# Attention by head pairs in eight slots of the input projection, in a two-layer encoder step on one core

## The chip, the cores and the metric

One Trainium2 chip, one of its cores. The time is the device time of one execution in microseconds (us), the median of several runs. Engines go by the names of the profile: PE (TensorE, its weight loads apart as PEld), DVE (VectorE), ACT (ScalarE), POOL (GpSimd), SP (SyncE, which issues the weight loads).

## What is computed

One step of a hybrid encoder for 256 prompt frames and 64 sample frames, 320 columns together, each of 1,024 numbers. Layer 0 runs two kinds of attention behind one input projection, layer 1 a matrix memory; both have a gated convolutional feed-forward part and an embedding. All is float32. The change lies in layer 0's attention and in the start of the program:

```python
def att_mixer(h, w_in, fox_fb, swa_sink, w_out, fox_cache, swa_cache):
    qa, ka, va, fa, qb, kb, vb = split_cols(h @ w_in, ATT_SIZES)
    logf = jax.nn.log_sigmoid(fa.astype(jnp.float32) + fox_fb.astype(jnp.float32))
    if fox_cache is None:
        oa = fox_prompt(qa, ka, va, logf)
        ob = swa_prompt(qb, kb, vb, sink)
    else:
        oa = fox_sample(qa, ka, va, logf, fox_cache[0], fox_cache[1], fox_cache[2])
        ob, sk, sv = swa_sample(qb, kb, vb, sink, swa_cache[0], swa_cache[1])
    out = jnp.concatenate([oa.reshape(b, S, FOX_HEADS * HEAD_DIM), ob], axis=-1) @ w_out
```

Forgetting attention (fox, 8 heads of 64) is causal softmax attention to whose scores F_q - F_k is added, F being the running sum of logf over cache and frames. Sliding-window attention (swa, 8 query heads on 2 key heads) sees a band of chunks of 64 frames, and its softmax has a sink term in the sum. For the prompt the keys are the prompt's; for the sample a cache of 256 (fox) or 128 (swa) rows comes in front.

## The kernel before, in words

One function, `encoder_step`, holds a block of code for each engine; the engines run through their own lists and wait for each other on counted semaphores. Weights come as units of 128 output columns (512 KB): SP loads unit u into one of four buffers, ACT copies it to a high part (`hi`, L1120), DVE subtracts to get a low part (`lo`, L1399), and PE multiplies in three terms, eight blocks of three matmuls with 320 columns (`block3`, L626 to L628). 270 units make up nearly all of the time.

At the start SP loads the tokens and the first units, ACT and POOL load parameters, caches and embeddings. PE turns the tokens (L690), DVE copies them, ACT and DVE split them (`prenorm`, L1124, and `prenorm_lo`, L1403). `ahead` (L650, L653) runs the first three units block by block behind these, since normalization is applied to the result. `stats` (L668) sums the squares, POOL takes the root (`inverse_rms`, L526), DVE and PE spread it over the columns, and DVE scales the units as it reads them (`in0_read`). The narrow projection (8 columns, weights `wnr`) gives the forget values.

`attention_events` sets the order of the attention on all engines: 48 tasks, one for each kind, head and row tile (two of 128 prompt rows, one of 64 sample rows). A task is `scores` (PE, L854, and L856 for the term of F), the move of the scores with a mask to SBUF and their maximum on DVE (`scores_moved`, L1496 to L1505), the exponential on ACT (`weights`, L1147), the reciprocal sum on DVE and the scaling on POOL or DVE (L552, L1514), transposes on PE three tasks later (`turn`, L880), their copy on ACT (L1157), and `values` (PE, L897) two tasks after that. Projection units 0 to 11 run before the first task; units 12 to 17 are cut in halves and stand between the first 21 tasks; `out_blocks` starts two units of the output projection at the last task. `turn_tok` (L830) turns keys and values for the outputs, `sum_forget` (L809) makes the running sums F on PE. Before unit 4 to 9, `TURNS_AT` places the turns of parameters (`par`), embeddings (`pe`), the narrow projection, and the caches (L768).

The groups that go through PSUM banks 0 to 3 take turns in the order of `group_order`; a group waits until the one four places ahead is read.

## Time and profile before

| | us |
|---|---|
| median of 3 runs | 1197.88 |
| lowest and highest | 1193.0, 1198.23 |
| the profiled execution | 1189.34 |
| span of the profile | 1187.6 |
| PE busy | 1151.6 (97%) |
| PEld busy | 1078.8 (91%) |
| DVE busy | 706.1 (59%) |
| ACT busy | 550.5 (46%) |
| POOL busy | 270.6 (23%) |

The span runs from the first to the last instruction. PE's busy time counts matmuls from start to modelled end, so that they overlap; the distance from one start to the next is the better measure of one. PEclk is the granted clock of TensorE as a share of 2.4 GHz.

### The profile page before, as it was taken

What the parts mean: (1) busy time and instruction counts of PE and PEld (TensorE: products, weight loads), DVE (VectorE), ACT (ScalarE), POOL (GpSimd) and SP (SyncE); (2) the same over time, 40 slices, a digit from 0 to 9 for tenths busy, and PEclk for the clock granted to TensorE, in tenths of its full rate; (3) what the DMA queues carried; (4) which work ended last, traced back from release to release, by engine and by line L of the source; (5) the groups of instructions that cost most, each with busy time, mean ns of one, the idle gap of its engine ahead of it and who ended that gap; (6) DMA issues with size and microseconds to landing.
All of it is one profiled execution on the core that took longest, in us unless ns stands there. A gap on an engine that the chain in (4) does not pass through costs nothing.

```text
span 1187.6 us, 20938 instructions
## 1 busy us (share of the span) xinstructions
PE 1151.6 (97%) x7495; PEld 1078.8 (91%) x7495; DVE 706.1 (59%) x1312; ACT 550.5 (46%) x972; POOL 270.6 (23%) x390
## 2 busy tenths in 40 slices
PE   4999999999999999999999999989999999999998
PEld 3887768899999999999998967789999999999998
DVE  4666653577777775333586546547777777633364
ACT  4244443545555554333462554455555455433343
POOL 5002223422232222000230200234222233200020
PEclk9999967899999999999998999989999999999999
DMA  9431102435555555445355432453555555554541
GB/s 240 127 107 54 54 1 74 120 106 159 169 149 144 156 145 155 146 148 154 107 151 134 108 89 60 80 131 95 166 160 154 147 151 149 149 154 145 157 118 52
DMA packets 283656, 150.41 MB, mean 127 GB/s; under 512 B 7576, under 2 KB 280272, under 8 KB 283600
## 3 DMA queue, kind: packets, MB, share of 16 engines
q1 hardware_dynamic: 278832, 144.20, 42.5%
q0 software_dynamic: 2384, 5.26, 1.9%
q8 instruction: 38, 0.62, 0.2%
q10 hardware_dynamic: 2384, 0.18, 0.2%
q14 instruction: 18, 0.15, 0.0%
HBM read 145.54 MB, written 4.08 MB: 126 GB/s over the span
## 4 chain that ended last, share of the span: by engine, by line
PE 90%; DVE 5%; DMA 2%; ACT 1%; issue 1%; POOL 0%; SPq 0%; ACTq 0%; DVEq 0%
PE bank L626 25%; PE bank L628 24%; PE bank L627 24%; PE bank L854 2%; PE bank L897 2%; PE bank L650 2%; DMA raw<-in_w_att_in 2%; PE bank L653 1%; PE bank L880 1%; PE bank L985 1%; DVE hL L1403 1%; DVE wl L1399 1%; PE bank L668 1%; PE bank L999 1%; ACT wh L1120 1%
## 5 line engine op out<-in xcount | busy, mean ns | idle before, releaser
L1399 DVE TENSOR_TENSOR wl<-raw,wh 128x1024 fp32r<-128x1024 f32 x270 | 333.1, 1234 | 260.5 <-ACT wh L1120 258.3
L626 PE MATMUL bank<-hH,wh 128*128 128x320 f32 x1272 | 399.8, 314 | 0.6 <-ACT Vaug L1271 0.5
L628 PE MATMUL bank<-hH,wl 128*128 128x320 f32 x1272 | 393.9, 310 | 0.0
L627 PE MATMUL bank<-hL,wh 128*128 128x320 f32 x1272 | 393.7, 310 | 0.0
L1120 ACT ACTIVATE wh<-raw 128x1024 fp32r<-128x1024 f32 x270 | 284.3, 1055 | 212.8 <-PE bank L628 186.6
L626 PEld LDWEIGHTS bank<-hH,wh 128*128 128x128 f32 x1272 | 239.5, 188 | 8.0 <-issue 4.5
L627 PEld LDWEIGHTS bank<-hL,wh 128*128 128x128 f32 x1272 | 239.7, 188 | 0.1
L628 PEld LDWEIGHTS bank<-hH,wl 128*128 128x128 f32 x1272 | 239.5, 188 | 0.0
L626 PE MATMUL bank<-hidden_hi,wh 128*128 128x320 f32 x720 | 225.0, 313 | 1.3 <-DVE hidden_lo L1791 1.2
L627 PE MATMUL bank<-hidden_lo,wh 128*128 128x320 f32 x720 | 223.5, 310 | 0.0
L628 PE MATMUL bank<-hidden_hi,wl 128*128 128x320 f32 x720 | 223.4, 310 | 0.0
L626 PEld LDWEIGHTS bank<-hidden_hi,wh 128*128 128x128 f32 x720 | 136.0, 189 | 3.0 <-DVE hidden_lo L1791 1.3
L627 PEld LDWEIGHTS bank<-hidden_lo,wh 128*128 128x128 f32 x720 | 136.2, 189 | 0.0
L628 PEld LDWEIGHTS bank<-hidden_hi,wl 128*128 128x128 f32 x720 | 136.1, 189 | 0.0
L605 POOL TENSOR_TENSOR fb<-cv,us 128x256 f32<-128x256 f32 x64 | 44.3, 691 | 313.8 <-DVE us L1833 198.3
L394 POOL TENSOR_TENSOR sqb<-sqb 128x320 f32<-128x320 f32 x42 | 42.2, 1004 | 207.4 <-ACT sqb L1340 146.0
L1325 ACT ACTIVATE cv<-cv 128x322 f32<-128x322 f32 x64 | 30.4, 474 | 100.8 <-DVE cv L1828 100.8
L1828 DVE SCALAR_TENSOR_TENSOR cv<-gp,PC,cv 128x322 f32<-128x322 f32 x128 | 70.5, 551 | 7.6
L1329 ACT ACTIVATE hidden_hi<-fb 128x320 f32 (+1 forms) x64 | 30.2, 472 | 79.4 <-POOL cs L609 79.4
L609 POOL COPY cs<-gp 128x4 f32 x64 | 63.0, 985 | 0.0
L1837 DVE TENSOR_TENSOR hidden_lo<-fb,hidden_hi 128x320 f32 (+1 forms) x64 | 31.3, 490 | 44.3 <-ACT hidden_hi L1329 44.3
L1322 ACT ACTIVATE cv<-gp,PC 128x322 f32<-128x322 f32 x64 | 42.2, 659 | 22.8 <-DVE gp L1820 20.9
(340 smaller groups left out, 1243.7 us busy)
## 6 DMA issues: line engine op xcount, KB each, us to landing
raw<-in_w_ffn_up SPq DMA_DIRECT2D x128, 512.0 KB, 4.0
raw<-in_w_ffn_down SPq DMA_DIRECT2D x64, 512.0 KB, 4.0
raw<-in_w_rec_in SPq DMA_DIRECT2D x24, 512.0 KB, 3.9
raw<-in_w_att_in SPq DMA_DIRECT2D x18, 512.0 KB, 4.1
raw<-in_w_ple_gate SPq DMA_DIRECT2D x16, 512.0 KB, 4.1
raw<-in_w_att_out SPq DMA_DIRECT2D x8, 512.0 KB, 3.8
raw<-in_w_rec_out SPq DMA_DIRECT2D x8, 512.0 KB, 3.9
raw<-in_w_ple SPq DMA_DIRECT2D x4, 512.0 KB, 3.5
```

The costliest lines, as they stand in the source:

```text
L394: ops.tensor_tensor(sqb[:, 0, :], sqb[:, 0, :], sqb[:, j, :], ALU.add).then_inc(sem("sq_added"), 1)
L605: g.tensor_tensor(fb[:, s, 0:TP], cv[:, s, 0:TP], us[:, s, 0:TP], ALU.mult)
L609: g.tensor_copy(dst, tail).then_inc(sem(f"f{l}"), 1)
L626: mmul(out, a, rh[:, k, :], start=first and k == 0, stop=False)
L627: mmul(out, a, rl[:, k, :], start=False, stop=False)
L628: m = mmul(out, b, rh[:, k, :], start=False, stop=last and k == 7)
L1120: A(wh[:, u % R, :], raw[:, u % R, :], ACT.Copy).then_inc(hi_ready, 1)
L1322: A(cv[:, s, :], gp[:, s, 2:T + 4], ACT.Identity, scale=PC[:, l, bass.ds(j + 64, 1)], bias=PC[:, l, bass.ds(j + 96, 1)]).then_inc(sem(f"cv ...
L1325: A(cv[:, s, :], cv[:, s, :], ACT.Gelu_apprx_tanh).then_inc(sem(f"gelu{l}"), 1)
L1399: V.tensor_tensor(wl[:, u % R, :], raw[:, u % R, :], wh[:, u % R, :].bitcast(F32), ALU.subtract).then_inc(lo_ready, 1)
L1828: V.scalar_tensor_tensor(out=cv[:, s, :], in0=gp[:, s, tap:tap + T + 2], scalar=PC[:, l, bass.ds(j + 32 * tap, 1)], in1=cv[:, s, :], op0=A ...
L1837: V.tensor_tensor(FL[:, bass.ds(j, 1), :].rearrange("p a t -> p (a t)"), fb[:, s, :], FH[:, bass.ds(j, 1), :].rearrange("p a t -> p (a t)" ...
```

## The change

Units are put in another order: keys and values of the swa heads, then their queries, then query, key and value of each fox pair (`ATT_COLS`). The attention has eight slots, one for a pair of heads, swa first (s = 0 to 3), and in each both heads, the two prompt tiles and the sample rows are done at once. The events are `u` (a whole projection unit), `S` (scores), `norm` (scaling), `PT` (turned weights), `PV` (values), `o` (the output split), `vt` and `kt` (values and keys turned), `lf` (forget values). Score banks are 4, 5 (prompt rows of the two heads) and 6 (sample rows of both, with the queries in a block-diagonal tile `QB`, which POOL writes); values use bank 7. DVE moves a slot's scores in five pieces with one operation each, which adds the mask, turns the sign and keeps the minimum. The swa sink is no extra column any more, but a term of the sum. F comes from scans on DVE, and F_q is left out, since softmax does not change by it; the term of F_k is put into the banks ahead of the scores.

At the start, `ahead` takes two units; ACT does all its splits before the squares; POOL makes its constants first and begins its loads when weight unit 2 has landed, the two narrow weights and layer 0's convolution parameters among them, which ACT loaded before. The root of the first normalization stands on POOL in the middle of the loads. PE runs 16 matmuls on constants before the tokens land, and three behind each token tile from the fourth on. Three output units instead of two are started in the last slots, block by block in the order of `K_ORDER`.

```diff
-ATT_COLS = [P * j for j in range(12)] + [1544 + P * j for j in range(6)]
+ATT_COLS = [2056, 2184] + [1544 + P * p for p in range(4)] + [512 * j + P * p for p in range(4) for j in range(3)]
...
-SKEW_T, SKEW_V = 3, 5
...
-HALF_AT = [0, 2, 4, 6, 8, 10, 12, 14, 16, 18, 19, 20]
-TOK_AT = [1, 2, 3, 21, 24, 25]
...
-OUT_FROM = len(TASKS) - 1
+FIRST = 2
+WARM = 16
+
+
+K_ORDER = [4, 5, 6, 7, 0, 1, 2, 3]
...
+    e = [("par", 0), ("par", 2), ("par", 3), ("cache", 4), ("u", 4), ("pe", 0), ("pe", 1), ("u", 5),
+         ("S", 0), ("pe", 2), ("pe", 3), ("vt", 0), ("u", 6), ("norm", 0), ("narrow", 0), ("cache", 0), ("cache", 1),
+         ("PT", 0), ("S", 1), ("u", 7), ("norm", 1), ("PV", 0), ("cache", 2), ("cache", 3), ("o", 0), ("u", 8),
+         ("PT", 1), ("S", 2), ("lf", 0), ("u", 9), ("norm", 2), ("PV", 1), ("vt", 1), ("o", 1), ("u", 10)]
+    for s in range(2, 6):
+        e += [("PT", s), ("S", s + 1), ("u", 2 * s + 7), ("norm", s + 1), ("PV", s)]
+        e += [("vt", (0, 0, 0, 2, 3, 4)[s])] if s > 2 else []
+        e += [("o", s)] + ([("u", 2 * s + 8)] if s < 5 else [])
+    e += [("kt", 0), ("kt", 1), ("PT", 6), ("S", 7), ("kt", 2), ("kt", 3), ("kt", 4)]
+    e += [("out", k) for k in range(4)] + [("norm", 7), ("PV", 6), ("o", 6), ("out", 4), ("out", 5), ("PT", 7), ("out", 6), ("PV", 7), ("o", 7)]
+    return e
...
+def group_banks():
+
+    fixed = {("pt_e", 7): 4, ("pt_o", 7): 5, ("pt_s", 7): 6}
+    fixed.update({("o", s): 7 for s in range(8)})
+    banks, turn, last, previous = [], 0, {}, []
+    for n, key in enumerate(group_order()):
+        b = fixed.get(key)
+        if b is None:
+            b, turn = turn % 4, turn + 1
+        banks.append(b)
+        previous.append(last.get(b))
+        last[b] = n
+    return banks, previous
...
+            link(g.memset(MS[:], 0.0))
+            link(g.tensor_copy(MS[0:64, TP:T], MFox[0:64, 256:320]))
+            link(g.tensor_copy(MS[64:128, TP:T], MFox[64:128, 320:384]))
+            g.memset(QB[:], 0.0)
...
+            g.memset(gp[:], 0.0).then_inc(sem("const2"), 1)
+
+            def inverse_rms(stage):
+                pool.wait_ge(sem("ms"), NORMS[stage] + 1)
+                g.tensor_tensor(rcol[:], ms[:], cst[:, 2:5], ALU.pow).then_inc(sem("rcol"), 1)
+
+            par0, par, ld_pe, ld_cache = sem("ld_par0"), sem("ld_par1"), sem("ld_pe"), sem("ld_cache")
+            pool.wait_ge(raw_landed[2], 16)
+            for i, nm in enumerate(("w_att_in", "w_rec_in")):
+                c = (1536, 2048)[i]
+                pool.dma_start(wnr[:, i], I[nm][0][:, c:c + 8].rearrange("(k p) c -> p k c", p=P)).then_inc(sem("ld_narrow"), 16)
+            pool.dma_start(prow[0:96, 0, :], I["ffn_conv_w"][0].rearrange("t (j c) -> (t j) c", c=P)).then_inc(par0, 16)
...
+            inverse_rms("mixpre0")
...
+            for i in range(WARM):
+                mmul(bank[7][:, 0:P], ones[:], ident[:], start=True, stop=True)
...
+                if j >= 3:
+                    for i in range(3):
+                        mmul(bank[7][:, 0:P], ones[:], ident[:], start=True, stop=True)
...
+                ahead([UNITS["in0"] + i for i in range(FIRST)], [gid("in0", i) for i in range(FIRST)], hH, hL,
+                      *prenorm_waits("mixpre0"))
+                in_unit(0, 2, lambda k: stats("mixpre0") if k == 5 else None)
+                in_unit(0, 3, rms_at("mixpre0", 6))
...
+                    elif name in ("vt", "kt"):
+                        turn_tok(name, i)
+                    elif name == "S":
+                        scores(i)
+                    elif name == "PT":
+                        turn_weights(i)
+                    elif name == "PV":
+                        values(i)
+                    elif name == "out":
+                        out_blocks(0, i)
+                for at in range(7):
+                    out_block(0, 2, at)
+                out_blocks(0, 7)
+                out_block(0, 2, 7)
+
+            def turn_cache(j):
+
+                gi = gid("cache", j)
+                bank_free(pe, gi)
+                pe.wait_ge(sem("ld_cache"), 16 * 6)
+                for t in range(2 if j < 4 else 1):
+                    m = trans(gbank(gi)[:, t * P:(t + 1) * P], kcache[:, t, j * P:(j + 1) * P] if j < 4 else kcs[:], ident[:])
+                m.then_inc(done(gi), 1)
...
+                    trans(gbank(gi)[0:n, t * 8:t * 8 + 8], lfz[0][:, t0:t0 + n], ident[0:8, 0:8])
+                for t in range(2):
+                    m = trans(gbank(gi)[0:8, 64 + t * P:64 + (t + 1) * P], clf[:, t, :], ident[:])
+                m.then_inc(done(gi), 1)
...
+            def scores(s):
+
+                fox, p = s > 3, s % 4
+                if s:
+                    pe.wait_ge(sem("s_moved"), 5 * s)
...
+                    for t in range(2):
+                        for half in range(2):
+                            hf, h = 64 * half, 2 * p + half
+                            mmul(bank[4 + half][:, t * P:t * P + (t + 1) * P], selR[hf:hf + 40, h:h + 1].to_broadcast([40, P]),
+                                 FrowR[hf:hf + 40, 0:(t + 1) * P], start=t == 0, stop=False, skip_group_check=True)
+                    mmul(bank[6][:, 0:T], selS[:, 2 * p:2 * p + 2, :].rearrange("p a b -> p (a b)"), FrowR[0:40, TP:TP + T],
+                         start=True, stop=False, skip_group_check=True)
+                for t in range(2):
+                    for half in range(2):
+                        hf = 64 * half
+                        m = mmul(bank[4 + half][:, t * P:t * P + (t + 1) * P], q[hf:hf + 64, t * P:(t + 1) * P], k[hf:hf + 64, 0:(t + 1) * P],
+                                 start=not fox and t == 0, stop=True, skip_group_check=True)
+                        if t:
+                            m.then_inc(sem("s_done"), 1)
+                pe.wait_ge(sem("queries"), 2 * s + 2)
+                mmul(bank[6][:, 0:w], QB[:, s, :], kc, start=not fox, stop=True, skip_group_check=True)
+                mmul(bank[6][:, w:w + TS], QB[:, s, :], k[:, TP:T], start=False, stop=True, skip_group_check=True).then_inc(sem("s_done"), 1)
...
+            def turn_weights(s):
+
+                b = s % 2
+                for half in range(2):
+                    gi = gid(("pt_e", "pt_o")[half], s)
...
+                    pe.wait_ge(sem("p_ready"), 5 * s + 2 * half + 2)
+                    for i, c in enumerate((0, P, 2 * P)):
+                        m = trans(gbank(gi)[:, i * P:(i + 1) * P], S_sb[:, b, 384 * half + c:384 * half + c + P], ident[:])
+                    m.then_inc(done(gi), 1)
...
+            def values(s):
+
...
+                for t in range(2):
+                    for half in range(2):
+                        hf, W = 64 * half, (PTe, PTo)[half]
+                        mmul(gbank(gi)[hf:hf + 64, t * P:TP], V[:, t, c[half]:c[half] + 64], W[:, 2 * t * P:2 * t * P + (2 - t) * P],
+                             start=t == 0, stop=t == 1)
...
+            def weights(s):
+
+                b = s % 2
+                for i, (_, _, c, w) in enumerate(pieces(s)):
+                    act.wait_ge(sem("s_moved"), 5 * s + i + 1)
+                    A(S_sb[:, b, c:c + w], S_sb[:, b, c:c + w], ACT.Exp, scale=-1.0, bias=nmax[:, b, i:i + 1],
+                      accum_out=aden[:, b, i:i + 1]).then_inc(sem("s_exp"), 1)
...
+                    A(hH[:, j, :], xT[:, j, :], ACT.Copy, scale=NC[:, 0, 64 + j:65 + j]).then_inc(sem("h_hi"), 1)
+                    if j == 3:
+                        hi(1)
...
+                for j in range(KT):
+                    A(sqb[:, j, :], xT[:, j, :], ACT.Square).then_inc(sem("sq"), 1)
+                    if j == 3:
+                        hi(3)
...
+            def scores_moved(s):
+
+                fox, b = s > 3, s % 2
...
+                masks = [MFox[:, 2 * P:], MFox[:, P:]] * 2 + [MS[:]] if fox else [MSwa[:, P:], MSwa[:]] * 2 + [MFox[:, 0:P + TS]]
+                for i, (bk, c0, c, w) in enumerate(pieces(s)):
+                    if i % 2 == 0:
+                        dve.wait_ge(sem("s_done"), 3 * s + i // 2 + 1)
+                    V.tensor_tensor_reduce(out=S_sb[:, b, c:c + w], in0=bank[bk][:, c0:c0 + w], in1=masks[i], scale=-1.0,
+                                           scalar=3e38 if fox else nsink5[:, s, i:i + 1], op0=ALU.add, op1=ALU.min,
+                                           accum_out=nmax[:, b, i:i + 1]).then_inc(sem("s_moved"), 1)
...
+            def normalise(s):
+
+                b = s % 2
+                dve.wait_ge(sem("s_exp"), 5 * s + 5)
...
+                V.reciprocal(ainv[:, b, :], aden[:, b, :]).then_inc(sem("a_inv"), 1)
+                dve.wait_ge(sem("a_inv"), 2 * s + 2 if s < 4 else s + 5)
+                for i, (_, _, c, w) in enumerate(pieces(s)):
+                    V.tensor_scalar(S_sb[:, b, c:c + w], S_sb[:, b, c:c + w], ainv[:, b, i:i + 1], None, ALU.mult).then_inc(sem("p_ready"), 1)
```

The first place is POOL's list at the start (`DMA` is the issue of a transfer; `clf` and `sinkb` are the last of six cache loads, `gp` the last constant, `rcol` the root). Before:

```order
L498 DMA clf<-in_cache_fox_logf 128x2x8
L499 DMA sinkb<-in_swa_sink 128x8
L501 MEMSET Ut 128x128
L502 AFFINE_SELECT Ut<-Ut 128x128 [waits const_step]
...
L515 MEMSET gp 128x648 [waits const_step]
L526 TENSOR_TENSOR rcol<-ms,cst 128x3 [waits ms]
L521 DMA out_s_swa_k<-kcs 64x128 [waits ld_cache]
```

Now:

```order
L508 MEMSET gp 128x648 [waits const_step]
L518 DMA wnr<-in_w_att_in 128x8x8 [waits raw_landed2]
L518 DMA wnr<-in_w_rec_in 128x8x8
L519 DMA prow<-in_ffn_conv_w 96x128
...
L526 DMA nrow<-in_rec_norm 8x128
L512 TENSOR_TENSOR rcol<-ms,cst 128x3 [waits ms]
L529 DMA petok<-in_p_prompt 128x2x256
...
L538 DMA clf<-in_cache_fox_logf 128x2x8
L539 DMA sinkb<-in_swa_sink 128x8
L545 DMA out_s_swa_k<-kcs 64x128 [waits ld_cache]
```

The constants stand ahead of the loads, the loads begin behind a wait for weight unit 2, and the root has moved from behind all of them to a place ahead of 13: four of embeddings (`petok`), three of biases and six of caches, in their old order.

The second place is PE's list where projection unit 3 ends and unit 4 begins (`prow`, `nrow` are parameter rows, `kcs` the swa key cache). Before:

```order
L702 MATMUL bank<-ident,prow 128x128 [waits in_read0,ld_par1]
L702 MATMUL bank<-ident,nrow 128x104 [waits in_read0]
L626 MATMUL bank<-hH,wh 128x320 [waits lo_ready,in_read0]
L627 MATMUL bank<-hL,wh 128x320
L628 MATMUL bank<-hH,wl 128x320
```

Now:

```order
L732 MATMUL bank<-ident,prow 128x128 [waits in_read0,ld_par0]
L732 MATMUL bank<-ident,prow 128x128 [waits in_read0,ld_par1]
L732 MATMUL bank<-ident,nrow 128x104 [waits in_read0]
L826 MATMUL bank<-ident,kcs 128x128 [waits ld_cache,in_read0]
L656 MATMUL bank<-hH,wh 128x320 [waits lo_ready,par_in]
L657 MATMUL bank<-hL,wh 128x320
L658 MATMUL bank<-hH,wl 128x320
```

The turn of the key cache, with its wait for the cache loads, has moved ahead of unit 4; it stood ahead of unit 9, with the same wait ahead of unit 8.

The third place is PE's list amid the fox heads (`S_sb` are weights to be turned, `FrowR` and `selR` or `selS` give the term of F, `hH` and `wh` belong to a projection unit). Before, the small matmuls of several tasks stood between two halves of a unit:

```order
L830 MATMUL bank<-ident,kT 128x128 [waits in_read0,tok_read]
L830 MATMUL bank<-ident,kT 128x128 x3
L854 MATMUL bank<-kT,mix 128x128 [waits s_moved]
L856 MATMUL bank<-FrowR,selR 128x128
L880 MATMUL bank<-ident,S_sb 128x128 [waits p_ready]
L830 MATMUL bank<-ident,kT 64x128 [waits in_read0,tok_read]
L830 MATMUL bank<-ident,kT 64x128 x3
L854 MATMUL bank<-kT,mix 128x256 [waits s_moved]
L856 MATMUL bank<-FrowR,selR 128x256
L626 MATMUL bank<-hH,wh 128x320 [waits lo_ready,in_read0]
L627 MATMUL bank<-hL,wh 128x320
L628 MATMUL bank<-hH,wl 128x320
```

Now the last turns of slot 4 and all scores of slot 5, with a whole unit behind them:

```order
L904 MATMUL bank<-ident,S_sb 128x128 [waits p_ready,vt_read]
L904 MATMUL bank<-ident,S_sb 128x128
L905 MATMUL bank<-ident,S_sb 64x128
L874 MATMUL bank<-FrowR,selR 128x128 [waits in_read0,s_moved]
L874 MATMUL bank<-FrowR,selR 128x128
L874 MATMUL bank<-FrowR,selR 128x256 x2
L876 MATMUL bank<-FrowR,selS 128x320
L881 MATMUL bank<-kT,mix 128x128 x2
L881 MATMUL bank<-kT,mix 128x256 x2
L886 MATMUL bank<-kcT,QB 128x256 [waits queries]
L887 MATMUL bank<-kT,QB 128x64
L656 MATMUL bank<-hH,wh 128x320 [waits lo_ready,in_read0]
```

The matmuls of one slot now stand together, with a wait at their head and one ahead of `QB`.

## Rows read from the trace of the kernel before

**Rows 1.** Busy by stage: stretch, its length, then each engine's busy us, PEclk, DMA share.

```profile
42.80:82.00 39.20, 39.13 (x270) 35.56 (x270) 23.56 (x43) 12.04 (x13) 1.29 (x2) 1.00 0.45 120
82.00:143.00 61.00, 60.32 (x384) 45.73 (x384) 39.35 (x98) 30.57 (x89) 11.35 (x15) 1.00 0.24 70
143.00:157.00 14.00, 12.70 (x81) 8.10 (x81) 9.98 (x46) 8.53 (x36) 4.89 (x7) 1.00 0.01 3
157.00:190.00 33.00, 33.00 (x123) 20.53 (x122) 15.54 (x68) 12.96 (x58) 10.03 (x14) 0.50 0.01 5
...
221.50:238.40 16.90, 13.90 (x76) 12.65 (x74) 13.56 (x22) 9.29 (x21) 11.11 (x11) 0.80 0.21 62
```

**Rows 2.** The chain that ended last, its beginning: start us, us, what.

```profile
3.84 17.98 DMA raw<-in_w_att_in
...
24.30 0.87 PE bank L650 x2
...
37.41 1.81 POOL rcol L526
...
42.84 0.42 PE bank L626
...
221.61 1.37 PE bank L668 x12
```

**Rows 3.** Timeline of PE, one weight block of an output unit: start us, us.

```profile
198.13 0.31 PE L626 MATMUL bank<-hidden_hi,wh 128*128 128x320 f32 x1
...
198.57 0.31 PE L626 MATMUL bank<-hidden_hi,wh 128*128 128x320 f32 x1
```

**Rows 4.** Timeline of PE, attention matmuls among projection blocks.

```profile
84.14 0.48 PE L854 MATMUL bank<-kT,mix 64*128 64x128 f32 x2
84.38 0.30 PE L856 MATMUL bank<-FrowR,selR 40*128 40x128 f32 x1
...
86.57 0.70 PE L854 MATMUL bank<-kT,mix 64*128 64x256 f32 x2
86.92 0.47 PE L856 MATMUL bank<-FrowR,selR 40*128 40x256 f32 x1
87.32 0.66 PE L830 MATMUL bank<-ident,kT 128*128 128x128 f32 x4
87.91 0.64 PE L854 MATMUL bank<-kcT,mix 64*64 64x256 f32 x2
...
110.66 0.27 PE L897 MATMUL bank<-PT,Vtok 64*64 64x64 f32 x1
110.67 0.43 PE L854 MATMUL bank<-kcT,mix 64*64 64x256 f32 x1
```

**Rows 5.** Groups of DVE by shape, 41 to 222 us (busy us, mean ns | idle before).

```profile
L1399 DVE TENSOR_TENSOR wl<-raw,wh 128x1024 fp32r<-128x1024 f32 x24 | 29.5, 1228 | 21.4 <-ACT wh L1120 21.4
...
L1505 DVE TENSOR_REDUCE amax<-S_sb 128x1 f32<-128x256 f32 x8 | 3.4, 420 | 0.3
...
L1501 DVE TENSOR_TENSOR S_sb<-bank,MSwa 128x256 f32<-128x256 f32 x8 | 3.3, 413 | 0.0
...
L1590 DVE TENSOR_TENSOR peL<-pef,peH 128x1280 fp32r<-128x1280 f32 x1 | 1.5, 1492 | 0.0
```

**Rows 6.** Timeline of POOL, the first and last of 13 load issues.

```profile
6.23 0.77 POOL L489 DMA_DIRECT2D petok<-in_p_prompt  x1
...
13.58 0.56 POOL L499 DMA_DIRECT2D sinkb<-in_swa_sink  x1
```

**Rows 7.** DMA issues of 0 to 60 us: KB each, us to landing.

```profile
wnr<-in_w_rec_in ACTq DMA_DIRECT2D x1, 32.0 KB, 15.3
...
out_s_swa_v<-vcs POOLq DMA_DIRECT2D x1, 32.0 KB, 2.8
...
sinkb<-in_swa_sink POOLq DMA_DIRECT2D x1, 4.0 KB, 7.0
```

More of the change, by code:

```diff
@@ L638, in unit @@
                         hook(k)
-                    block3(u, k, out, rh, rl, first, last)
+                    block3(u, k, out, rh, rl, first and k == 0, last and k == 7, k == 7)
             def ahead(us, gs, rh, rl, hi_wait, lo_wait):
@@ L1455, in narrow @@
                 s = sem(f"narrow_step{l}")
-                scaled(l, 0, z[:, 0, :], rows=slice(0, 8), last=False, name=f"narrow{l}").then_inc(s, 1)
+                scaled(l, 0, z[0], rows=slice(0, 8), last=False, name=f"narrow{l}").then_inc(s, 1)
                 dve.wait_ge(s, 1)
@@ L1727, in input_recurrent @@
                     elif name == "narrow":
-                        narrow(1, mz)
+                        narrow(1, [mz[:, i, :] for i in range(3)])
                     elif name == "half":
```

819 lines of the change are left out of this document (368 added, 451 removed).

## The prediction

> **What bounds the kernel now.** The profiled execution took 1189.34 us by its own clock, 1187.6 us of it span; the three timed runs have a median of 1197.88 us, 8.5 us more. I sum against the profile and put the difference on the median. A change of 0.5% (6 us) is about the least that a measurement of this kernel can tell from none.
>
> I read the busy times by stage first, because the change lies wholly between the start and the sum of squares behind the first output projection. From 42.80 to 190 us TensorE is called busy almost throughout [rows 1], but two things are to be seen. In the stretch from 82 to 143 us its weight loads fall far behind its matmuls, since the small attention matmuls come between the projection's. And once projection blocks have run out, TensorE has gaps (12.70 of 14 us busy), and in the next 33 us the granted clock is 0.50, the lower level of 1.2 GHz [rows 1]. So the attention stage is bound by TensorE's own instruction list, half of the time at half speed; VectorE is busy 39.35 of 61 us there, and is not the bound.
>
> Then the chain that ended last, at its beginning [rows 2]: it hangs on a weight transfer that lands at 21.84 us, passes to TensorE at 24.30, to the root on GpSimd at 37.41, to the fifth projection unit at 42.84, and reaches the sum of squares of the output projection at 221.61. The stretch that the change rewrites is therefore 221.61 - 42.84 = 178.8 us, with the start ahead of it.
>
> **Part 1: the start.** The loads of GpSimd's queue, some 2 MB, now wait until weight unit 2 has landed. Before, the tokens, three units and these loads, 4.8 MB, took the 17.98 us of the chain's transfer [rows 2], 0.27 MB per us. The tokens and two units are 2.25 MB: 8.4 us by that rate, so both are there at some 12 us. FIRST = 2 needs no third unit. Behind ScalarE's copy and the split of 1.23 us [rows 5] on VectorE, I put the first projection matmul at 14.5 us instead of 24.30. Before, from there to the start of the root was 13.1 us, with three units in front of it. The changed order has two units, five blocks of the third, then the sum of squares, which waits a little for its additions; I take 12.2 us, and with the root's 1.81 us [rows 2] it ends at 28.5 us, 10.7 us sooner.
>
> But this gain is not kept. GpSimd now issues the last 13 loads behind the root, and TensorE wants the turned sliding-window cache, which waits for all six cache loads, ahead of unit 4 (before, this wait stood ahead of unit 8). The same 13 issues took from 6.23 to 14.14 us [rows 6], 7.9 us, so the last goes out at 36.4. It needs 2.8 us at least (a small store in a quiet stretch) and 7.0 at most (the same load when the queues were full) [rows 7]; the queues then carry four weight units beside it, so I take 4.2. Unit 4 starts at 40.8 us, 2.0 us sooner; bounds 39 and 44. TensorE stands idle from about 33 to there. In the stretch from 221.5 us, which also holds an idle engine, the mean clock was 0.80 of 16.9 us [rows 1], 3.4 us lost, so between 0 and 3.4 us is lost behind this wait; I take 2. **The start comes to nothing: -2.0 + 2 = 0**, with ends -4 and +5. The warming matmuls on TensorE cost nothing: nothing can run there before the tokens land. The two narrow weight loads move from ScalarE's queue to GpSimd's, behind unit 2, and VectorE waits for them ahead of the mean square; before they needed up to 15.3 us [rows 7], with full queues. Issued at 13 to 16 us they land between 17 and 30; only past 24 do they delay the root. That makes the upper end +5 rather than +1. The constants, now ahead of the loads on GpSimd, are done before unit 2 lands.
>
> **Part 2: the work from unit 4 on.** All of it is TensorE's list, at full clock. A block of three is 0.44 us [rows 3], so a unit of 24 is 3.53; 14 input and 8 output units are 77.6 us, unchanged. 50 transposes (embeddings, caches, keys and values) at 0.59/4 = 0.15 [rows 4] are 7.5, the narrow projection 24 x 0.147 = 3.5, the turned forget values 0.8: 11.8 together. The 15 forget sums on TensorE go; the three scans that replace them run on VectorE, where a whole slot covers them.
>
> A slot: scores of 128 columns cost 0.24, of 256 columns 0.35, a row-sum matmul of 256 columns 0.40 [rows 4]; 64 columns have no row and lie between 0 and 0.24, I take 0.20; values go by the same widths. A banded slot: scores 2 x 0.24 + 2 x 0.35 + 0.24 + 0.20 = 1.62, eight transposes 1.20, values 2 x 0.35 + 2 x 0.24 + 4 x 0.20 = 1.98; 4.8 us. A forget slot: row sums 2 x 0.24 + 2 x 0.40 + 0.45 = 1.73, scores 1.73, nine transposes 1.35, values 1.18 + 6 x 0.20 = 2.38; 7.2 us. Four of each: **48.0 us**.
>
> The two heads of a pair use different halves of the array's rows. Twice at full clock a matmul on 64 rows begins with its neighbour: 110.66 and 110.67 us [rows 4]. So part of each pair overlaps; I take off 4 us, between 0 and 10. TensorE: Matmul & The Clock Gate in the Trainium skill, section "Why this matters for your kernels", says that small matmuls in distinct row groups, or in distinct column groups, run at the same time; by it the values would overlap as well, and this is the second rival.
>
> Hand-overs between units and attention I put at 3 us, from none to 6.
>
> Stalls: a slot's scores are moved by five fused operations on VectorE. The row does not exist before; for 256 columns it costs at least the plain move, 0.41, and at most move and reduction, 0.83 [rows 5]. Taking 0.5 on average, 2.5 us, the exponentials follow behind, the unit's read and split take 2.9 us after the unit, the scaling 2.0: weights are ready some 7.5 us after the scores. TensorE has 3.53 + about 2 + 0.45 + 3.53 = 9.5 us of other work there, so nothing is lost; at 0.83 per piece, 9.1, still covered. GpSimd's copies of queries and doubled keys are needed 10 us after the cache wait and take 4. One place is not covered: slot 0's weights. Behind its scaling VectorE still has the split of the embeddings, 1.49 us [rows 5], the four narrow steps and two cache copies, and the banks of the second and third turn are freed by these: 8.5 us of VectorE after unit 6, against 4.1 + 0.4 on TensorE. 4 us stall, between 1 and 8; 1 us more for the rest. The tail is covered too: slots 6 and 7 have key turns and output blocks between them.
>
> Sum: 77.6 + 11.8 + 48.0 - 4 + 3 + 5 = 141.4 us in place of 178.8: **-37.4 us**. With the start at 0 the profile would be 1152 us, the median 1160.5. The ends are from -47 (start -4, overlap 10) to -19 (start +5, no overlap, 4 us more of stalls, hand-overs +3, and 2 us of VectorE in the slots).
>
> Where it comes from: half clock in 33 us [rows 1] lost 16.5; the 48 attention tasks, at full clock, took the rest of the stretch, 178.8 - 16.5 - 77.6 - 14 = 70.7 us (14 for the turns, the narrow projection and some 2 us of forget sums), against 48.0 - 4 + 5 + 3 = 52.
>
> **Rivals.** *The caches come later.* If the narrow weights land past 24 us, or the last load needs 7 us, unit 4 starts at 47, the clock loss is 3.4, and the first slot waits 8. For it: every load is issued behind one on the same queue, and the root stands between. Against it: far less traffic at that time. 6.2 + 1.4 + 4 = 12 us more than forecast: 1172. Chance 0.17.
>
> *Pairs run wholly together.* Scores and values of two heads at once: per banded slot 0.59 + 1.0 less, per forget slot 0.59 + 0.64 + 1.2; 16 us in all, where I took 4. Time 1148.5. For it: the shared starts [rows 4]; against it: consecutive value matmuls in the rows of before never show it. Chance 0.17. By the rule of that page the row and the column halves would overlap, and this is what it would give.
>
> *The clock falls and stays, slower than before.* Place: the idle before unit 4, then the many waits in slots. Price: work at 1.2 GHz takes twice its time, so each us spent at half speed costs half of it. It decides from 2 x 37 = 74 us spent at the lower level between 41 and 185 us; 100 us of it gives 1211. For it: it fell after 14 us with 1.3 us of gaps [rows 1]. Against it: there were no projection blocks then, while from 82 to 143, where they are interleaved as now, it stayed at 1.00. Chance 0.05.
>
> *The slots do not shorten anything*, because stalls fill what TensorE saves: within 6 us of before. Chance 0.03; nothing in VectorE's load speaks for it.
>
> **How the numbers follow.** My forecast (1151 to 1169, chance 0.58) gives 1160.5. To hold the time 8 times in 10 the range goes from 1145, which takes in the overlapping pairs, to 1179, past the late caches. Faster by over 0.5%: 0.58 + 0.17 + 0.17 = 0.92; same 0.03; slower 0.05.
>
> **What would show it.** In the changed profile: the first projection matmul near 14.5 us; the root near 28; a gap on TensorE from 33 to 41 put down to the cache load, with a fall of the clock behind it; a stall of some 4 us at slot 0's turned weights; clock at 1.00 from 50 us to the sum of squares; that sum near 185 instead of 221.61. Wrong would be: a gap elsewhere of over 3 us, half clock inside the slots, a fused move over 1 us, or unit 4 before 36 us.

## The result, and the profile after

The changed kernel takes 1137.65 us (median of 4 runs, 1137.24 to 1139.77); the kernel before, beside it, 1197.86 (1193.0 to 1198.23). The ratio on record is 0.9534, 95% interval 0.9479 to 0.9588; the kernel before spreads by several us (see the last experiment), and the quotient of these two medians alone is 0.9497. The forecast was 1160.5, its range 1145 to 1179: the direction was right, and the time lies 7 us below the range. The profiled execution took 1137.24 us, 52.1 less than the one before; the forecast for it was 37.4 less.

The busy times by stage of the changed kernel, to be held against [rows 1] (stretch, its length, then each engine's busy us, the granted clock, DMA share, GB/s):

```profile
33.50:42.20 8.70, 0.52 (x3) 0.50 (x3) 2.92 (x6) 0.00 (x0) 3.52 (x7) 0.70 1.11 305
42.20:50.00 7.80, 7.80 (x37) 7.33 (x37) 3.62 (x13) 1.06 (x1) 4.05 (x12) 0.67 0.07 19
...
58.00:66.70 8.70, 6.03 (x43) 4.17 (x41) 6.47 (x16) 3.04 (x5) 0.47 (x2) 1.00 0.27 72
66.70:80.00 13.30, 13.28 (x92) 11.97 (x94) 7.87 (x27) 8.72 (x20) 0.00 (x0) 0.87 0.15 41
80.00:95.00 15.00, 15.00 (x120) 13.55 (x119) 12.54 (x40) 9.44 (x31) 1.74 (x4) 1.00 0.32 84
95.00:110.00 15.00, 14.98 (x123) 13.42 (x123) 10.45 (x30) 8.32 (x27) 1.40 (x2) 1.00 0.32 94
110.00:127.00 17.00, 17.00 (x140) 15.45 (x138) 10.71 (x32) 8.46 (x24) 0.46 (x2) 1.00 0.32 93
127.00:150.00 23.00, 21.00 (x180) 18.40 (x179) 10.53 (x40) 11.28 (x41) 4.68 (x8) 1.00 0.37 113
```

The 33 us at 0.50 are gone: from 80 us to the sum of squares the clock is 1.00. What is left is a hole ahead of 42 us, a mean clock of 0.67 behind it, a smaller hole at 58 to 66.7 us with a clock of 0.87 behind it, and 2 us without work between 127 and 150 us. The chain that ended last shows the first two holes, and answers to [rows 2] (start us, us, what):

```profile
26.94 1.80 POOL rcol L512
...
36.14 5.45 DMA sinkb<-in_swa_sink
...
41.73 0.45 PE bank L826
42.18 0.29 PE bank L656
...
63.38 1.40 DVE peL L1617
...
66.33 0.34 DVE kcT L1645
...
66.72 0.33 PE bank L904
```

The root ends at 28.74, the last load goes out at 36.14, lands 5.45 later, and unit 4 begins at 42.18. In slot 0 the embeddings' split and a cache copy stand ahead of the third turn. The sum of squares of the output projection, at 221.61 in [rows 2], begins at 172.57.

| | forecast | measured |
|---|---|---|
| first projection matmul | 14.5 | 15.95 |
| root ends | 28.5 | 28.74 |
| unit 4 begins | 40.8 | 42.18 |
| from there to the sum of squares | 141.4 + 2 | 130.4 |
| from there to the end of the span | 966.0, as before | 962.8 |

One fox slot of the changed kernel on TensorE's timeline (start us, us; each score or value matmul of the program shows up as two passes, and a row is one pass or several that follow each other):

```profile
112.87 0.82 PE L897 MATMUL bank<-ident,S_sb 128*128 128x128 f32 x6
...
113.95 0.50 PE L874 MATMUL bank<-FrowR,selR 40*128 40x128 f32 x4
...
114.29 0.95 PE L881 MATMUL bank<-kT,mix 64*128 64x128 f32 x8
115.17 0.70 PE L886 MATMUL bank<-kcT,QB 128*128 128x256 f32 x2
...
115.84 0.40 PE L656 MATMUL bank<-hH,wh 128*128 128x320 f32 x1
...
119.54 0.43 PE L920 MATMUL bank<-PTe,Vtok 128*64 128x256 f32 x1
119.55 0.43 PE L920 MATMUL bank<-PTo,Vtok 128*64 128x256 f32 x1
...
120.24 0.40 PE L932 MATMUL bank<-PTs,vcache 128*64 128x64 f32 x8
...
120.83 0.44 PE L847 MATMUL bank<-ident,sqb 128*128 128x128 f32 x2
```

The first passes of the two heads' values begin 0.01 us apart, as the two matmuls at 110.66 and 110.67 us do in [rows 4]. The slot takes 115.84 - 112.87 = 2.97 and 120.83 - 119.54 = 1.29, together 4.26 us; the forecast had 7.2 before its deduction for overlap. A banded slot, measured in the same way, takes 2.28 + 1.18 = 3.46, against 4.8.

### The profile page after: what moved, and what is told of

The parts are those of the page before. It is cut to its first block, busy times and chain, and to the rows that moved or that the text cites. A ratio compares the mean times of both kernels' runs of the same rounds, so it can differ in the third digit from the quotient of the medians.

```text
span 1135.4 us, 20638 instructions
## 1 busy us (share of the span) xinstructions
PE 1101.6 (97%) x7433; PEld 1056.6 (93%) x7433; DVE 689.1 (61%) x1274; ACT 540.8 (48%) x932; POOL 258.1 (23%) x386
## 4 chain that ended last, share of the span: by engine, by line
PE 90%; DVE 5%; ACT 2%; POOL 1%; issue 1%; DMA 0%; ACTq 0%; DVEq 0%; POOLq 0%
PE bank L656 26%; PE bank L658 25%; PE bank L657 25%; PE bank L680 2%; PE bank L683 1%; PE bank L1020 1%; DVE hL L1437 1%; ACT wh L1151 1%; DVE wl L1433 1%; PE bank L698 1%; PE bank L1034 1%; PE bank L720 1%; DVE xT L1467 1%; DVE hidden_lo L1910 1%; PE bank L706 1%
```

## Experiments

Two lengths are compared throughout: the moment at which VectorE takes the mean square of the output projection (223.0 us in the kernel before, 174.0 in the changed one), which closes the rewritten stretch, and the length of layer 1's mixer from its first mean square to the one behind its output projection (171.6 and 168.5 us), whose instructions no version touches.

| kernel | median us (lowest to highest) | mean square at | layer 1's mixer |
|---|---|---|---|
| changed | 1137.65 (1137.24 to 1139.77) | 174.0 | 168.5 |
| heads apart | 1143.82 (1141.91 to 1146.37) | 177.5 | 170.0 |
| same half | 1153.34 (1152.27 to 1154.34) | 187.9 | 171.6 |
| units ahead | 1153.19 (1152.51 to 1153.88) | 190.6 | 168.5 |
| moved twice | 1146.6 (1146.5 to 1147.25) | 182.7 | 168.5 |
| no warming | 1137.65 (1137.08 to 1141.21) | 174.9 | 171.6 |
| caches first | 1131.27 (1130.03 to 1134.31) | 168.6 | 168.5 |
| slot 0 freed | 1142.13 (1141.62 to 1144.12) | 175.6 | 173.1 |
| slot 0 freed, caches in twos | 1136.25 (1136.24 to 1138.32) | 169.9 | 171.6 |
| caches first, unit 4 first, slot 0 freed | 1123.05 (1122.01 to 1128.62) | 159.1 | 168.5 |

### Do the two heads of a pair run at the same time?

First the heads one behind the other, in row sums, scores and values alike:

```diff
-                for t in range(2):
-                    for half in range(2):
+                for half in range(2):
+                    for t in range(2):
```

> Same instructions as the changed kernel, but in scores, row sums and values of a slot all matmuls of the first head stand ahead of those of the second, so that neighbours use the same half of the array. Theory A (the neighbours of a pair run at the same time, and that is what the forecast priced too low): the prompt's values cost 0.71 us more per slot, the sample's about 0.4, the scores about 0.3 (2 x 0.24 + 2 x 0.35 = 1.18 one after the other, against 0.86 in the changed kernel's trace); 1.2 to 1.6 us in each of eight slots, 10 to 13 us in all: 1147 to 1151 us, and no two value matmuls begin within 0.02 us of each other. Theory B (the small matmuls are cheap in any order, and the rows of before were too dear because TensorE waited there for its weight loads): 1137 to 1140 us.

Measured: 1143.82 us, and the mean square 3.5 us later. Both theories missed, and the timeline says why (a banded slot's values):

```profile
96.85 0.43 PE L920 MATMUL bank<-PTe,Stok 128*64 128x256 f32 x1
96.86 0.43 PE L920 MATMUL bank<-PTo,Stok 128*64 128x256 f32 x1
97.12 0.38 PE L920 MATMUL bank<-PTe,Stok 128*64 128x256 f32 x1
97.13 0.38 PE L920 MATMUL bank<-PTo,Stok 128*64 128x256 f32 x1
97.33 0.27 PE L920 MATMUL bank<-PTe,Stok 128*64 128x128 f32 x1
...
97.55 0.28 PE L932 MATMUL bank<-PTs,vcs 128*64 128x64 f32 x2
98.01 0.33 PE L932 MATMUL bank<-PTs,vcs 128*64 128x64 f32 x2
```

Here the program has PTe 256, PTe 128, PTo 256, PTo 128, and still PTo's first matmul begins with PTe's first, ahead of PTe 128 at 97.33 us. So the engine starts a matmul for the other column half although one for the first half is still waiting ahead of it. The prompt's values take 0.70 us in either order, the scores some 0.86; overlap was lost by the sample's values, 0.5 us in a banded slot (0.98 instead of 0.48) and 0.6 in a forgetting one (1.21 instead of 0.59), and by a forgetting slot's row sums, 0.13 us (0.47 instead of 0.34). Why the engine reached past the waiting matmul for the prompt's values and not for the sample's stays open. The order did not take the overlap of the rest away, so this run can't decide; the halves have to go.

The second run puts both heads on the same half, rows and columns (the attention's numbers are wrong by it, and two more matmuls on constants stand at the start, before the tokens land):

```diff
-                        hf = 64 * half
+                        hf = 0
...
-                        hf, W = 64 * half, (PTe, PTo)[half]
+                        hv, W = 64 * (s % 2), (PTe, PTo)[half]
...
-                        m = mmul(gbank(gi)[hf:hf + 64, TP:T], v, w, start=i == 0, stop=i == n)
+                        m = mmul(gbank(gi)[hv:hv + 64, TP:T], v, w, start=i == 0, stop=i == n, skip_group_check=True)
```

> The order of the changed kernel, but both heads of a pair use the same half of the array: scores and row sums of both read rows 0 to 63, values of both write one column half (the half of even slots is the first, of odd slots the second). The attention is therefore wrong in its numbers, with the same count and sizes of matmuls. In the run with the heads apart the prompt's values still began in pairs (96.85 and 96.86 us), and only the sample's lost their overlap. Theory A (matmuls in different halves run at the same time, whatever stands between them): now none overlap; the prompt's values go from 0.70 to 1.28 us per slot, the sample's from 0.5 to 1.0, the scores from 0.85 to 1.2, the row sums of a forgetting slot from 0.30 to at least 0.35: 1.4 to 1.6 us in each of eight slots, 10 to 13 us: 1148 to 1151 us, and each value matmul begins behind its neighbour. Theory B (small matmuls are cheap by themselves): under 3 us, as the 3.5 us of the run with the heads apart were hand-overs: 1137 to 1141 us.

Measured: 1153.34 us, the mean square 13.9 us later. Its fox slot, to be read against the one above:

```profile
121.59 0.82 PE L899 MATMUL bank<-ident,S_sb 128*128 128x128 f32 x6
...
122.67 0.72 PE L876 MATMUL bank<-FrowR,selR 40*128 40x128 f32 x4
...
123.38 1.47 PE L883 MATMUL bank<-kT,mix 64*128 64x128 f32 x8
...
125.46 0.39 PE L656 MATMUL bank<-hH,wh 128*128 128x320 f32 x1
...
129.15 0.65 PE L922 MATMUL bank<-PTe,Vtok 128*64 128x256 f32 x2
129.63 0.59 PE L922 MATMUL bank<-PTo,Vtok 128*64 128x256 f32 x2
...
130.50 0.63 PE L934 MATMUL bank<-PTs,vcache 128*64 128x64 f32 x8
...
131.43 0.55 PE L849 MATMUL bank<-ident,sqb 128*128 128x128 f32 x3
```

Every part that pairs is longer: row sums with the sample's 0.71 instead of 0.34, the prompt's scores 1.40 instead of 0.88, the prompt's values 1.35 instead of 0.70, the sample's 0.93 instead of 0.59. The slot takes 3.87 + 2.28 = 6.15 us against 4.26, a banded one 2.94 + 2.05 = 4.99 against 3.46. All these parts stand at full clock. Four of each make 13.7 us; from unit 4 to the sum of squares this kernel takes 143.3 us against 130.4, 12.9 more. Theory A holds: the overlap is shown, and is worth 13 to 14 us. The time lies 2.3 us above the theory's range; the profiles are 17.1 us apart, of which 3.1 lie in layer 1's mixer (more below) and 1.05 in a later unit 4. One rival for the values: on the same column half both heads also add into the same place in PSUM. For the scores they do not (banks 4 and 5), and these lost their overlap too; and the projection's matmuls, which all add into one place, follow each other at 0.147 us [rows 3], so a common place alone holds nothing up there.

### What spreading the units is worth

```diff
+    us = [x for x in e if x[0] == "u" and x[1] > 5]
+    e = [x for x in e if x not in us]
+    at = e.index(("S", 0))
+    return e[:at] + us + e[at:]
```

> The twelve projection units that stand between the slots all run ahead of slot 0; the slots follow without them. Theory A (the spreading is what hides the way from scores over VectorE, ScalarE and back, 5 to 7 us for each slot, and what holds the clock up): TensorE has some 4.3 us of its own work per slot and waits 2 to 5 us in each, 16 to 40 us in all, and the granted clock falls to 0.50 in the slots: 1155 to 1185 us. Theory B (the gain comes from the pairing alone, and two slots in flight are enough cover): 1137 to 1143 us.

Measured: 1153.19 us, just under theory A's range. Its stages, where the slots now stand alone:

```profile
110.00:130.00 20.00, 15.38 (x90) 10.83 (x91) 12.64 (x54) 11.44 (x46) 2.99 (x8) 0.59 0.01 1
130.00:150.00 20.00, 18.33 (x144) 14.05 (x143) 12.54 (x52) 11.23 (x44) 0.00 (x0) 0.78 0.01 2
```

TensorE has gaps of 4.6 and 1.7 us and a clock of 0.59 and 0.78: the picture of [rows 1] from 143 us on, made by the order alone. At these clocks at most 0.41 x 20 + 0.22 x 20 = 12.6 us are lost, and 9.5 if all the gaps fell into the time at half speed, since idle time gets no longer by a lower clock. So more than half of the 15.5 us that the spreading is worth (16.6 at the mean square) is clock, and the rest is waiting.

### How much VectorE's fused move is covered

```diff
+                    V.tensor_tensor(S_sb[:, b, c:c + w], bank[bk][:, c0:c0 + w], masks[i], ALU.add).then_inc(sem("s_added"), 1)
+                    dve.wait_ge(sem("s_added"), 5 * s + i + 1)
                     V.tensor_tensor_reduce(out=S_sb[:, b, c:c + w], in0=bank[bk][:, c0:c0 + w], in1=masks[i], scale=-1.0,
```

> Ahead of each fused move of scores stands a plain addition of mask and scores to the same tile, so that VectorE does what a plain move and a fused one would cost: 5 x about 0.38 us = 1.9 us more per slot, 15 us more of VectorE. Theory A (the forecast's: 9.5 us of TensorE's work cover some 7.5 us from scores to weights): only slots 0, 6 and 7, which have less work ahead, wait for it, 2 us each: 1138 to 1144 us. Theory B (the fused move is what made the slots fit): every slot waits, 10 to 15 us: 1147 to 1153 us.

Measured: 1146.6 us, between the two ranges; the mean square 8.7 us later. In the changed kernel the fused move takes, by shape (busy us, mean ns | idle before):

```profile
L1528 DVE CUSTOM_DVE_ANT_0 S_sb<-bank,MSwa,nsink 128x256 f32<-128x256 f32 x8 | 3.8, 481 | 0.0
L1528 DVE DVE_READ_ACCUMULATOR2_ANT nmax<- 128x1 f32 x40 | 3.4, 84 | 0.0
L1528 DVE CUSTOM_DVE_ANT_0 S_sb<-bank,MFox 128x256 f32<-128x256 f32 x8 | 3.4, 421 | 0.0
```

So a piece of 256 columns costs 0.51 to 0.57 us with the reading of its minimum, inside the bounds of the forecast, 0.41 and 0.83. The sum of the forecast did not rest on the cover, as the fused move came out near the value taken. With the move done twice, one of TensorE's waits from unit 4 to the sum of squares is this (two places):

```profile
PE bank L897 <- DVE S_sb L1548: 2.4, 2, 1.2
```

All of them come to some 9.3 us, against 4.7 in the changed kernel: 1.20, 1.86 and 0.84 at slot 0's turns, 1.14 ahead of slot 4's row sums, 1.22 at slot 6's turns, 2.81 ahead of an output block in the tail, and 0.28 ahead of the narrow projection. So the waits stand where theory A put them, but for slot 4; the cover of the slots between held. What theory A left out is the clock behind the waits, 0.80 from 58 to 75 us and 0.91 from 127 to 150 us.

### The start

The warming matmuls left out (two loops removed):

> The 16 matmuls on constants ahead of the tokens and the three behind each token tile are left out; everything else stands. Theory A (they hold the clock up for the first units, and because the last loads stand behind the root, a later root means a later unit 4): the first units run at 0.27 instead of 0.147 us per matmul for some 2 to 5 us, root, last load and unit 4 come as much later: 1139 to 1142 us. Theory B (TensorE idles 8.2 us ahead of unit 4 in any case, and the turns of the tokens hold the clock as well): within 1 us of 1137.6 us.

Measured: 1137.65 us, the same median as with them, as theory B has it. Theory A's mechanism is there and its price isn't. The first matmuls run at half clock (1.36 us for four, where the changed kernel has 0.58), and the root moves (the chain, start us, us):

```profile
15.22 1.36 PE bank L680 x4
...
28.48 1.80 POOL rcol L512
...
43.03 0.45 PE bank L821
```

The root is 1.54 us later and the sliding-window cache's turn 1.30, but the mean square only 0.9. The rest was made good on the way, and layer 1's mixer scatters by more than that.

Then the cache loads ahead of the root on GpSimd's queue:

```diff
+            pool.dma_start(kcache[:], I["cache_fox_k"][0, 0].rearrange("(t p) h d -> p t (h d)", p=P)).then_inc(ld_cache, 16)
...
+            pool.dma_start(sinkb[:], I["swa_sink"][0:1, :].to_broadcast([P, NH])).then_inc(ld_cache, 16)
             inverse_rms("mixpre0")
             for l in range(2):
```

> The six cache loads stand on GpSimd's queue behind the parameters and ahead of the root, instead of behind root, embeddings and biases. Theory A (unit 4 waits for nothing but the last cache load, 8.2 us, and the fall of the clock behind it costs 2.5): unit 4 starts near 34 instead of 42.2 us, at full clock; 10 to 11 us less, 1126 to 1129 us. Theory B (the queues are full in that stretch, and cache loads that go earlier push the weight units back, or the embeddings are late instead): unit 4 or the embeddings' turns wait for another transfer, and 4 us at most are gained, 1133 to 1137 us.

Measured: 1131.27 us, 6.4 less, between the theories. The wait for the load is gone, but other waits stood behind it (the waits of TensorE from 20 to 75 us: what waited, for what, us in total):

```profile
PE bank L897 <- DVE us L1480: 1.7, 1, 1.7
PE bank L826 <- DVE mix L1482: 1.2, 1, 1.2
PE bank L656 <- DVE PC L1565: 1.0, 1, 1.0
```

Unit 4 begins at 36.05 instead of near 34, behind VectorE's reads of the banks, and not at full clock (0.80 from 33.5 to 42.2 us); and behind slot 0's waits the clock fell to 0.61 from 58 to 66.7 us, where the changed kernel has 1.00, and 0.87 only in the stage behind.

Slot 0's weights freed by later places for the embeddings' copy and split and the first two forgetting cache turns:

```diff
-         ("S", 0), ("pe", 2), ("pe", 3), ("vt", 0), ("u", 6), ("norm", 0), ("narrow", 0), ("cache", 0), ("cache", 1),
-         ("PT", 0), ("S", 1), ("u", 7), ("norm", 1), ("PV", 0), ("cache", 2), ("cache", 3), ("o", 0), ("u", 8),
+         ("S", 0), ("pe", 2), ("pe", 3), ("vt", 0), ("u", 6), ("norm", 0), ("narrow", 0),
+         ("PT", 0), ("S", 1), ("u", 7), ("norm", 1), ("PV", 0), ("cache", 0), ("cache", 1), ("cache", 2), ("cache", 3), ("o", 0), ("u", 8),
```

> The first two forgetting cache turns stand behind slot 0's values, the embeddings' copy on ScalarE behind slot 1's turned weights and their split on VectorE behind slot 2's scaling, so that neither stands ahead of slot 0's weights. Theory A (the waits of 1.7, 0.9 and 0.8 us at slot 0's turns come from VectorE's list, and the clock falls there for another 1 to 2 us): 3 to 5 us less, 1132.5 to 1134.5 us. Theory B (the scaling itself is the last thing, since it waits for the exponentials and a weight split in any case): within 1 us of 1137.6 us.

Measured: 1142.13 us, slower by 4.5, which neither theory had. Only part of that is the edit's: in the profile the mean square comes 1.6 us later, and 4.6 us lie in layer 1's mixer (173.1 against 168.5). The waits at slot 0 are gone, and one stands further on:

```profile
PE bank L656 <- DVE kcT L1648: 3.7, 1, 3.7
```

Unit 8 takes the bank of the first cache turn, which VectorE reads only behind slot 1's scaling. (Of the three waits that were expected to go, 1.7 and 0.9 us stood at slot 0's turns; the 0.8 us stands at slot 6's, at 134.7 us, and is still there.) With the copies in twos, behind slot 0's and slot 1's values (`("PV", 1), ("cache", 2), ("cache", 3)`), and the rest the same:

> The changed kernel with slot 0 freed as in the last version, its forgetting cache copies in twos behind slot 0's and slot 1's values, but loads and unit 4 where the change put them. Theory A (the first try lost the gain only because four cache groups in a row made unit 8 wait 3.7 us for a bank): waits of 2.6 us at slot 0's turns and the lower clock behind them go, nothing takes their place; to the sum of squares of the output projection 168 to 171 instead of 174.0 us, 1132 to 1135 us. Theory B (slot 0's own scaling comes no earlier, since it stands behind a weight split that waits for ScalarE): within 1 us of 1137.6 us.

Measured: the mean square at 169.9, 4.1 us earlier, as theory A has it; but the time is 1136.25, only 1.4 less. The profile loses 3.1 us again in layer 1's mixer, 171.6 instead of 168.5.

All three together, with unit 4 ahead of the turns:

```diff
-    e = [("par", 0), ("par", 2), ("par", 3), ("cache", 4), ("u", 4), ("pe", 0), ("pe", 1), ("u", 5),
+    e = [("u", 4), ("par", 0), ("par", 2), ("cache", 4), ("u", 5), ("par", 3), ("pe", 0), ("pe", 1),
```

> Caches ahead of the root as before, unit 4 ahead of the parameters' and the sliding-window cache's turns, and slot 0's weights freed from the embeddings' split and from the forgetting cache's copies, which now stand in twos behind slot 0's and slot 1's values. Theory A (with the caches early, three costs were left: unit 4 at 36.05 instead of some 32.5 us behind VectorE's reads, 2.7 us of waits at slot 0's turns, and the clock of 0.61 from 58 to 66.7 us behind them, 3.4 us): 7 to 10 us less than with the caches alone, 1121 to 1124.5 us. Theory B (each of these waits only moves to the next list, as the run with slot 0 freed alone showed, where unit 8 waited 3.7 us for the cache copies): 1128 to 1132 us.

Measured: 1123.05 us (1122.01 to 1128.62), ratio to the kernel before 0.9426, interval 0.9391 to 0.9461: faster than both kernels. Theory A holds; its stages where the holes were:

```profile
33.50:42.20 8.70, 8.44 (x60) 7.46 (x58) 7.23 (x20) 2.12 (x2) 6.43 (x13) 1.00 0.85 233
...
58.00:66.70 8.70, 8.42 (x72) 7.38 (x69) 6.45 (x20) 5.75 (x16) 0.00 (x0) 1.00 0.22 61
```

### Where the spread of the kernel before lies

> The kernel before, unchanged, for a second trace: its timed runs lie between 1185 and 1198 us, its trace was taken at 1189.34. The question is where its spread lies, since the forecast added the 8.5 us between trace and median to the changed kernel's time, whose own runs lie within 2.5 us. Theory A (the spread is the clock in the attention stretch, which falls at another moment from run to run): from unit 4 to the sum of squares of the output projection 178.8 us become 175 to 187, and the stages behind it keep their lengths within 3.1 us. Theory B (it is a fixed cost outside the span or in all stages): each stage is longer by the same share, at most 1%, or the span stays and only the time around it grows.

> The kernel before, unchanged, a third trace. As for the second: Theory A puts the difference of the times into the stretch from unit 4 to the sum of squares of the output projection (178.8 us in the first trace), Theory B into all stages or around the span.

> The changed kernel, unchanged, for a second trace. Its runs lie between 1137.2 and 1139.8 us. Theory A (its clock stays up in the attention, so only layer 1's mixer, which took 168.5 us in its trace, 170.0, 171.6 and 173.1 in traces of kernels with the same instructions there, can differ): the stretch from unit 4 to the sum of squares stays within 1 us of 130.4, and any difference of the times is layer 1's. Theory B: the attention's stretch spreads as well, by 2 us or more.

Measured: 1197.37 and 1192.32 us for the kernel before, 1140.06 for the changed one. The stage of [rows 1] from 143 to 157 us, in the second trace and then in the third:

```profile
143.00:157.00 14.00, 13.10 (x55) 7.91 (x54) 6.29 (x28) 5.76 (x23) 3.10 (x4) 0.56 0.01 4
```

```profile
143.00:157.00 14.00, 13.09 (x59) 8.30 (x59) 7.02 (x32) 6.71 (x28) 4.03 (x5) 0.64 0.01 2
```

In the first trace the clock was still 1.00 from 143 to 157 us [rows 1]; here it is 0.56 and 0.64. From the mean square at the start to the one behind the output projection the three traces take 185.8, 193.7 and 192.6 us, so theory A holds: most of the spread of the kernel before is the moment at which its clock falls in the last attention tasks. The third trace is also 3.2 us shorter in layer 1's mixer (168.4 us), which is why its time is only 3 us above the first's while its stretch is 6.8 us longer. The runs of the kernel before that were timed beside the experiments agree: they go from 1182.87 us at a mean clock of 0.983 to 1199.05 us at 0.967, with medians of 1192.87, 1193.28 and 1189.1. The changed kernel's second trace has its mean square at 173.7, within 0.3 us of the first; it is longer by 3.1 us in layer 1's mixer, 171.6 against 168.5, again as theory A has it.

## Why the prediction was wrong

**The start: right, in part by luck.** The first projection matmul came 1.45 us late, and from it to the start of the root 11.0 us passed where 12.2 were taken; the two misses nearly cancel, and the root ended 0.2 us from its place. The sum put the start at nothing, and unit 4 came 0.66 us earlier than before, 1.4 later than forecast: the load took 5.45 us where 4.2 was taken (bounds 2.8 and 7.0). The price of the idle engine behind it, taken as 2 us, shows as unit 4 in part at half clock, 5.9 us for 3.5. The hole, its releaser and the later place of the root were as named.

**The units: right.** From 80 to 127 us the clock is 1.00, and a unit with its hand-over takes 119.54 - 115.84 = 3.70 us where [rows 3] gave 3.53 without one. (The text of the prediction calls the stage "half of the time at half speed"; by [rows 1] it is 33 of the 147 us from 42.80 to 190, and the sums use the 33.)

**Slot 0's stall: right in place and kind,** 1.7 and 0.9 us at its turns, against 4 forecast between bounds of 1 and 8. Two things beside it were not forecast: the clock of 0.87 behind it, some 1.7 us, and waits of 0.8 and 1.2 us in the tail, which was called covered.

**The step that failed is "So part of each pair overlaps; I take off 4 us, between 0 and 10".** With the overlap taken away the eight slots cost 4 x (4.99 + 6.15) = 44.6 us; so the prices from [rows 4], 48.0 in all, were 3.4 too high: 1.05 too high in each forgetting slot (7.2 against 6.15, with row sums of 0.71 where 1.73 was taken), and 0.2 too low in each banded one. With it they cost 4 x (3.46 + 4.26) = 30.9. The overlap is 13.7, not 4: above its upper bound. This is the second rival, "Pairs run wholly together", with its 16 us; it had a chance of 0.17 because "consecutive value matmuls in the rows of before never show it". They could not: there consecutive value matmuls belong to one head and write one column half, so the rows were silent, not against. The rule that stood beside it (TensorE: Matmul & The Clock Gate in the Trainium skill, section "Why this matters for your kernels") agrees with these runs: values in two column halves 0.70 us, in one 1.35; scores in two row halves 0.88 us, in one 1.40. The terms together, 9.7 for the overlap and 3.4 for the prices, make up the 13.0 us by which the stretch from unit 4 came out shorter (130.4 against 143.4). That everything else in it comes to nearly nothing is a remainder, in which misses of both signs cancel: waits 4.7 us against 5, but lower clock some 4.1 against 2.

**The second failure is the step from the profile to the median, "8.5 us more".** The forecast carried it over as a fixed amount. In the kernel before it sits in the stretch that the change rewrites, as the two further traces show; the changed kernel's median is 0.4 us above its profile. That alone is 8.1 us. The size of the 8.5 was chance as well: against the three medians of the kernel before that were taken beside the experiments the same trace lies 3.5 and 3.9 us lower and 0.2 higher.

**Behind the stretch** the forecast left everything as it was, and the profile is 3.1 us shorter, all in layer 1's mixer, where the clock stayed up in this trace. It is no gain of the change: the second trace of the changed kernel has the 171.6 us of the kernel before, and the third trace of the kernel before has 168.4.

The account: 9.7 + 3.4 - 0.1 for the attention, -1.4 for the later unit 4, 3.1 for layer 1 and 8.1 for the median make 22.8 of the 22.9 us between 1160.5 and 1137.65; the -0.1 is the remainder named above.

**The rivals that fell:** the caches came 1.4 us later, not 6; the clock did not stay down (1.00 from 80 us to the sum of squares); and the slots did shorten. The clock's part of the forecast, 16.5 us for the 33 us at half speed, is supported by the run with the units ahead, which brings the fall back: 9.5 to 12.6 of its 15.5 us are clock, the rest waits, so it does not measure the 16.5.

## What to carry to other kernels

When a change puts two tasks side by side in different halves of the array, ask whether any row of the old kernel could have shown their overlap; where none could, the rows are no evidence against it, and the forecast should stand between the cases rather than near the one without. Before adding the distance between a profile and its median to a forecast, ask in which stage it arises, for it goes with that stage. A load that heads a critical stage should not stand on a queue behind work that waits for something else: the six cache loads ahead of the root, with unit 4 and slot 0 rearranged to use the time, took another 14.6 us off.

## What the hardware showed

Two things were not expected. TensorE started a matmul for one column half ahead of one for the other half that stood before it in the program: in the run with the heads apart PTo's first matmul begins at 96.86 us, while PTe's second, which stands ahead of it, begins at 97.33. And the same instructions of layer 1's mixer took 168.4 to 173.1 us in the traces of this study, in steps of about 1.5 us. The traces differ there in how long the clock was down. In the first 59 us of it, the changed kernel's first trace and the trace with slot 0 freed:

```profile
570.40:600.00 29.60, 28.34 (x198) 25.67 (x198) 19.64 (x44) 9.48 (x10) 5.47 (x10) 1.00 0.53 142
600.00:630.00 30.00, 30.00 (x218) 29.42 (x217) 18.80 (x53) 14.99 (x30) 8.43 (x12) 1.00 0.46 124
```

```profile
572.60:602.00 29.40, 28.14 (x181) 25.35 (x182) 18.84 (x43) 8.72 (x10) 5.46 (x10) 0.91 0.54 143
602.00:632.00 30.00, 30.00 (x202) 29.48 (x202) 17.75 (x51) 14.45 (x29) 8.45 (x12) 0.91 0.40 107
```

What decides in which run the clock falls there, or for how long, stays open: the kernels differ ahead of it only, and the two traces of the changed kernel differ in nothing but the run. Filling the waits ahead of these falls with matmuls was not tried.
